# A four-block fp32 network on one core: convolution taps spread differently, LayerNorm means read from PSUM and squares summed on DVE, and the order of ACT's and PE's work in the differential-attention heads

## The reference

```python
def even_layer(x, ...):                       # SSD + conformer convolution
    z_a, xbc, dt_raw, glu_v, glu_g, z_b = split(rmsnorm(x) @ w_in)
    xs, bs, cs = split(silu(causal_dwconv(xbc, conv_w, conv_b)))
    y_a = rmsnorm_by_group(ssd_chunked(xs, dt, a, bs, cs, d_skip) * silu(z_a))
    u = causal_dwconv(glu_v * sigmoid(glu_g), dw_w, dw_b)     # 31 taps
    y_b = silu(layernorm(u, ln_w, ln_b)) * silu(z_b)
    return x + concatenate([y_a, y_b]) @ w_out

def odd_layer(x, positions, ...):             # differential attention, 8 heads
    q, k, v, gate = split(rmsnorm(x) @ w_in)
    q, k = rotary(rmsnorm(q)), rotary(rmsnorm(k))
    # two softmaxes a head, block-causal; 128 query rows at a time
    pr = softmax(mask(q @ k.T * scale))
    o = (pr[0] - lam * pr[1]) @ v
    o = rmsnorm(o, subln_w) * (1 - lam_init) * silu(gate)
    return x + o @ w_out
```

## Time and profile before

| | |
|---|---|
| time, median of 3 runs (lowest to highest) | 3186.87 us (3180.26 to 3199.41) |
| time of the profiled execution | 3183.37 us |
| its span in the profile | 3181.6 us |
| busy: PE, DVE, ACT, POOL | 95%, 59%, 30%, 25% of the span |
| mean granted clock of PE, share of full speed | 0.987 |

### The profile page before, as it was taken

How to read it: one execution, slowest core, us unless ns; L and a number is a source line. 1 busy time by engine, 2 the same in 40 slices (tenths; PEclk the granted TensorE clock), 3 DMA queues, 4 the chain that set the end, 5 groups by cost and what they waited for, 6 DMA issues and landing times. The chain is left out here.

```text
span 3181.6 us, 40107 instructions
## 1 busy us (share of the span) xinstructions
PE 3031.9 (95%) x16111; PEld 2452.0 (77%) x16111; DVE 1889.3 (59%) x2778; ACT 952.0 (30%) x1839; POOL 809.3 (25%) x466
## 2 busy tenths in 40 slices
PE   7999999889999999999999999998999999999898
PEld 6778787777788888888777777776687777777677
DVE  5334666534654254354588889898534566676673
ACT  3232444324210000011333343333312344444431
POOL 3222000241433333333233333232132211111111
PEclk9999999999999999999999999999999999999999
DMA  3012000110211111112211211124131110000011
GB/s 128 33 34 97 14 1 15 34 60 27 66 46 46 53 46 53 53 46 76 77 47 43 78 54 67 54 67 179 59 96 65 34 34 27 27 27 27 29 59 67
DMA packets 49281, 170.37 MB, mean 54 GB/s; under 512 B 5200, under 2 KB 5472, under 8 KB 48224
## 3 DMA queue, kind: packets, MB, share of 16 engines
q1 hardware_dynamic: 49120, 168.15, 15.7%
HBM read 145.06 MB, written 23.07 MB: 53 GB/s over the span
## 5 line engine op out<-in xcount | busy, mean ns | idle before, releaser
L194 PE MATMUL acc<-x_hi,w_hi 128*128 128x512 f32 x2048 | 824.1, 402 | 39.4 <-POOL w_lo L189 16.4
L187 POOL CAST w_hi<-w_raw 128x1024 fp32r<-128x1024 f32 x217 | 239.8, 1105 | 2318.8 <-PE acc L196 1374.5
L196 PE MATMUL acc<-x_hi,w_lo 128*128 128x512 f32 x2048 | 801.4, 391 | 0.0
L195 PE MATMUL acc<-x_lo,w_hi 128*128 128x512 f32 x2048 | 800.5, 391 | 0.0
L189 POOL TENSOR_TENSOR w_lo<-w_raw,w_hi 128x1024 fp32r<-128x1024 f32 x217 | 549.2, 2531 | 17.4
L194 PEld LDWEIGHTS acc<-x_hi,w_hi 128*128 128x128 f32 x2048 | 386.5, 189 | 131.4 <-issue 38.0
L196 PEld LDWEIGHTS acc<-x_hi,w_lo 128*128 128x128 f32 x2048 | 385.9, 188 | 82.6
L195 PEld LDWEIGHTS acc<-x_lo,w_hi 128*128 128x128 f32 x2048 | 386.9, 189 | 77.1 <-issue 2.4
L2569 DVE SCALAR_TENSOR_TENSOR acc<-ev_upad,cols,acc 128x1024 f32<-128x1024 f32 x232 | 298.5, 1287 | 5.4
L194 PE MATMUL aux<-x_hi,w_hi 128*128 128x512 f32 x464 | 197.8, 426 | 0.6 <-POOL w_lo L189 0.6
L196 PE MATMUL aux<-x_hi,w_lo 128*128 128x512 f32 x464 | 184.0, 397 | 0.0
(11 more groups left out here) (512 smaller groups left out, 5043.2 us busy)
## 6 DMA issues: line engine op xcount, KB each, us to landing
w_raw<-in_stream SPq DMA_DIRECT2D x217, 512.0 KB, 3.5
h<-in_x SPq DMA_DIRECT2D x16, 512.0 KB, 9.1
spill_h<-h SPq DMA_DIRECT2D x8, 512.0 KB, 5.3
spill<-ev_zst SPq DMA_DIRECT2D x8, 512.0 KB, 4.0
h_even<-spill_h SPq DMA_DIRECT2D x8, 512.0 KB, 11.7
ev_bz<-spill SPq DMA_DIRECT2D x8, 512.0 KB, 3.4
spill_h<-h_even SPq DMA_DIRECT2D x8, 512.0 KB, 5.4
h<-spill_h SPq DMA_DIRECT2D x8, 512.0 KB, 4.3
```

Of the source, the lines that this page charges most:

```text
L187: pool.tensor_copy(k.w_hi[slot][:], k.w_raw[slot][:]).then_inc(k.w_split, 1)
L194: pe.matmul(out, w_hi, x_hi, start=start, stop=False)
L195: pe.matmul(out, w_hi, x_lo, start=False, stop=False)
L196: return pe.matmul(out, w_lo, x_hi, start=False, stop=stop)
```

## The change

In the even block's groups, `conv(g, 1, ...)` has no taps inside it and four after it. The last group has fewer taps in its early part and in its chunks, and more after them, so that 3 of them stand ahead of `add(0)`. `total` moves from the middle of tile 2 to its last quarter. The mean is no longer copied: the centring is a `scalar_tensor_tensor` that reads the sums in PSUM. DVE adds the eight squares into one tile, so that `total_squares` is 2 matmuls, now in the last quarter of tile 4 instead of behind tile 3. The inverse root is written to PSUM and read there.

In the heads ACT reads the `zb` bank ahead of both exponents, `turn_o(h - 1, 0)` stands one quarter earlier, and the silu of the gate moves from t = 3 to t = 7. The last head's output is split in two halves.

```diff
-                    if c and between is not None:
-                        between()
                     for q in range(KD):
+                        if c and q == 4 and between is not None:
+                            between()
                         if c == 0:
...
             def total_squares():
-                pe.wait_ge(s["mean"], 1)
-                for j in range(KD):
-                    pe.wait_ge(s["sq_done"], j + 1)
-                    for c in (0, 1):
-                        mm = pe.matmul(S[c], k.ones, sq[j][:, c * HALF:(c + 1) * HALF], start=j == 0, stop=j == KD - 1)
+                pe.wait_ge(s["centred"], KD)
+                pe.wait_ge(s["q_sum"], KD - 1)
+                for c in (0, 1):
+                    mm = pe.matmul(S[c], k.ones, sq[0][:, c * HALF:(c + 1) * HALF], start=True, stop=True)
                 mm.then_inc(s["total2"], 1)
...
             first_pair()
             for i in range(2, KD):
-                out_tile(i, x_hi, x_lo, nothing, total if i == 2 else None)
-                if i == 3:
-                    total_squares()
+                out_tile(i, x_hi, x_lo, nothing, {2: total, 4: total_squares}.get(i))
...
@@ -2498,15 +2495,13 @@
             last_high(0)
             last_high(1)

-            act.wait_ge(s["total"], 1)
-            act.activation(mu[:], aux[:, 0:SEQ], ACT.Copy, scale=1.0 / D).then_inc(s["mean"], 1)
             for j in range(KD):
                 act.wait_ge(s["centred"], j + 1)
...
-            act.activation(rstd[:], rstd[:], ACT.Exp, scale=-0.5).then_inc(s["root"], 1)
+            act.activation(aux[:, 0:SEQ], rstd[:], ACT.Exp, scale=-0.5).then_inc(s["root"], 1)
...
-                    conv(g, 1, True)
-                    taps(1)
+                    conv(g, 1, False)
...
+                last = g == SSD_GROUPS - 1
                 conv(g, 3, False)
-                taps(5)
+                taps(3 if last else 5)
                 arrive(8)
                 mix(g, 0)
                 arrive(LEAD - 8)
...
                 n = per_chunk(g)
                 for c in range(TT):
-                    short = g == SSD_GROUPS - 1 and c >= 3
-                    taps(2 if short else 3)
+                    taps(2 if last else 3)
...
                     arrive(n // 3)
                     combine(g, c)
                     add_y(g, c)
                     arrive(n // 3)
-                    taps(0 if short else 2)
+                    taps(1 if last and c != 4 else 2)
...
             last_multiply(0)
-            taps(4)
+            taps(6)
             last_multiply(1)
             taps(1)
             sum_squares(SSD_GROUPS - 1)
-            taps(3)
+            taps(5)
             normalise(SSD_GROUPS - 1)
...
-            taps(CONF_K * KD - done[0] - 4)
...
             add(0)
-            taps(4)
+            taps(CONF_K * KD)
...
-            dve.wait_ge(s["mean"], 1)
+            dve.wait_ge(s["total"], 1)
             dve.wait_ge(s["tap"], CONF_K * KD)
+
+            def sum_of(j):
+                dve.wait_ge(s["sq_done"], j + 1)
+                if j > 1:
+                    dve.wait_ge(s["q_sum"], j - 1)
+                dve.tensor_tensor(sq[0][:], sq[0][:], sq[j][:], ALU.add).then_inc(s["q_sum"], 1)
+
             for j in range(KD):
-                dve.tensor_tensor(uc[:, j, :], uc[:, j, :], mu[:], ALU.subtract).then_inc(s["centred"], 1)
-                if j == 3:
+                dve.scalar_tensor_tensor(uc[:, j, :], aux[:, 0:SEQ], -1.0 / D, uc[:, j, :], ALU.mult, ALU.add).then_inc(s["centred"], 1)
+                if j == 4:
                     add(2)
+                if j >= 2:
+                    sum_of(j - 1)
+            sum_of(KD - 1)
             add(3)
             dve.wait_ge(s["root"], 2)
             dve.wait_ge(s["centred"], KD)
             for j in range(KD + 2):
                 if j < KD:
-                    dve.tensor_tensor(uc[:, j, :], uc[:, j, :], rstd[:], ALU.mult).then_inc(s["scaled"], 1)
+                    dve.tensor_tensor(uc[:, j, :], uc[:, j, :], aux[:, 0:SEQ], ALU.mult).then_inc(s["scaled"], 1)
                 if 1 <= j <= KD:
...
+                if h >= 1 and t == 2:
+                    turn_o(h - 1, 0)
                 quarter(1)
                 if h >= 1 and t == 2:
-                    turn_o(h - 1, 0)
                     turn_o(h - 1, 1)
                 if own:
...
-            pe.wait_ge(s["od_lo"], 8)
-            for r in range(2):
-                for c in range(2):
+            for c in range(2):
+                pe.wait_ge(s["od_lo"], H + c)
+                for r in range(2):
                     mm = output(rows[r][c], 4, r, c, range(3, 4))
-                mm.then_inc(k.lin_done if r else s["pieces"], 1)
+                    if c:
+                        mm.then_inc(k.lin_done if r else s["pieces"], 1)
...
                     take(("zf", h + 1, t), zts[t % 2])
-                if nxt:
-                    exponent(*nxt, 0)
                 if z and 1 <= t <= 4:
                     key = ("zb", h + 1, t - 1)
                     wait_full(act, key)
                     used(act.activation(qk[(h + 1) % 2][:, :, 256 * (t - 1):256 * t],
                                         bank(key).rearrange("p (j c) -> p j c", j=2), ACT.Copy), key)
                 if nxt:
+                    exponent(*nxt, 0)
                     exponent(*nxt, 1)
+                if fill and t == TT - 1:
+                    silu_gate(h + 2)
                 if own:
...
                     evacuate(h + 2, t // 2, t % 2)
-                    if t == 3:
-                        silu_gate(h + 2)
...
-            split_output(H - 1)
+            for c in range(2):
+                cols = slice(c * HALF, (c + 1) * HALF)
+                act.wait_ge(s["ring_dve"], USE[("o", H - 1, c)][2])
+                act.activation(d_hi[:, H - 1, cols], o[:, H - 1, cols], ACT.Copy).then_inc(s["od_hi"], 1)
...
-            lower_output(H - 1)
+            for c in range(2):
+                cols = slice(c * HALF, (c + 1) * HALF)
+                dve.wait_ge(s["od_hi"], H + c)
+                dve.tensor_tensor(d_lo[:, H - 1, cols], o[:, H - 1, cols], d_hi[:, H - 1, cols].bitcast(F32), ALU.subtract).then_inc(s["od_lo"], 1)
```

More of the change, by code:

```diff
@@ L1966, in block_even @@
     b_z = k.at("ev_bz", 96, [P, KD, SEQ])
-    mu, sq = k.at("ev_mu", 96, [P, SEQ]), [k.at(f"ev_sq{i}", 100 + 4 * i if i < 7 else 132, [P, SEQ]) for i in range(KD)]
+    sq = [k.at(f"ev_sq{i}", 100 + 4 * i if i < 7 else 132, [P, SEQ]) for i in range(KD)]
     rstd, zr = k.at("ev_rstd", 128, [P, SEQ]), [k.at(f"ev_zr{i}", 132 + 4 * i, [P, SEQ]) for i in (0, 1)]
@@ L1980, in block_even @@
              "state_ready chain yadded z_gated ymul squared sq_sum gtotal groot ynormed y_hi y_lo y_spilled ya_back h_back h_back0 "
-             "ya_back1 ya_back2 ya_back3 ya_back4 ya_back5 total mean centred sq_done total2 root scaled silued z_back gated b_hi b_lo added").split()
+             "ya_back1 ya_back2 ya_back3 ya_back4 ya_back5 q_sum total centred sq_done total2 root scaled silued z_back gated b_hi b_lo added").split()
     s = {n: k.own(f"e_{n}") for n in names}
@@ L2718, in _ @@
                     arrive(8)
-                    conv(g, 1, True)
-                    taps(1)
+                    conv(g, 1, False)
+                    taps(4)
                     arrive(8)
@@ L2730, in _ @@
                 arrive(LEAD - 8)
-                taps(4)
+                taps(2 if last else 4)
                 n = per_chunk(g)
                 for c in range(TT):
-                    short = g == SSD_GROUPS - 1 and c >= 3
-                    taps(2 if short else 3)
+                    taps(2 if last else 3)
                     if c + 1 < TT:
@@ L2753, in _ @@
             last_low(1)
-            taps(CONF_K * KD - done[0] - 4)
+            taps(min(3, CONF_K * KD - done[0]))
             def add(i):
```

1 line of the change is left out of this document (removed).

## The result

The changed kernel takes 3150.06 us, the median of 4 runs (3148.32 to 3157.71); the kernel before took 3192.91 in the 4 runs beside it (3180.26 to 3199.41). The ratio is 0.9877, 95% interval 0.9855 to 0.9899, so 32 to 46 us less. Measured again with more runs, the ratio was 0.9897 (0.9865 to 0.9930). The profiled execution took 3151.43 with a span of 3149.6, against 3183.37 and 3181.6.

What follows compares the result with a forecast made beforehand. PE, busy 95% of the span, was taken as the bound. Gains of 5.7 + 15.6 + 13.6 + 1.5 + 1.6 + 1.8 = 39.8 took the profiled 3183.4 to 3143.6, set at 3145 for run spread; range 3131 to 3164.

Steps and rivals of the forecast that it cites:

- SSD, -5.7: Even block's groups: 4.0 us of waits go at L2151, 2.2 at L2175; taps put back return 0.5.
- Tile 2, -8.2: Even block's output tile 2: starts 8.2 us earlier, at 2220.0, once POOL's split weights are ready.
- Squares, 12.1: Even block's norm: 4 records of squares' sums in place of 32 save 12.1 us of PE's work.
- the root 13.4 earlier: Even block's norm: the inverse root comes at 2268.2 to 2268.5, 13.4 us earlier than before.
- 2.1 + 12.1 - 0.2 = 14.0: Tile 2 to tile 8: half clock gone 2.1, squares 12.1, less PE's 0.2 us wait for DVE's sums.
- The wait at tile 8, 4.6 and 2 of clock: Output tile 8: PE waits 4.6 us for weights loaded and split behind the root, then loses 2 to half clock.
- The split `b_lo` isn't it: Tile 8: DVE's splits also follow the root but don't bind, since PE needs them one by one, 0.7 us apart.
- Heads, -13.6, -1.5 and -1.6: Odd block: t = 4, 2.10 us waits and half clock go, 0.65 waits come; t = 2, -1.5; heads 0 and 6, -0.4 and -1.2.
- Silu, 0: Heads, t = 7: the silu's 3.66 us stretch and the copy behind it stay covered by 1.5 us; no change.
- Tail, -1.8: Last head's output in halves: PE starts at 3136.4 instead of 3138.13, 1.8 us less, ends 0.5 to 3.4.
- the 3.3 that I had taken: Even block's norm: 3.3 us allowed for DVE being slowed where POOL works beside it.
- The "slower" rival: Heads, t = 1 to 4: zb reads delay the exponents, 28 places at 1.9 us, 53 in all, about 3197; chance 0.04.

Runs made afterwards that it cites:

- the second profile: The changed kernel as it is, measured and profiled again: 3156.24 us, ratio 0.9897 to the kernel before.
- the run of the zb read alone: The kernel before with one edit, ACT reading the zb bank ahead of both exponents: 3171.71 us, ratio 0.9941 to the kernel before.
- the first experiment: The changed kernel with four taps moved out of the last group's chunks to behind add(0): 3136.76 us.

## Why the prediction was right, and where not

The forecast was 3145 with a range of 3131 to 3164, and a gain of 39.8 on the profiled execution; measured were 3150.06, a gain of 31.9 between the profiled executions and 39 by the ratio. By the stretches it is 33.0. The SSD missed by 8.3, and heads and tail gave 3.0 more than their 18.5; that the whole time still came within 5 us is partly luck, as the part ahead of the even block alone varies by 20. Term by term, by the stretches:

- **SSD, -5.7: wrong in sign.** The first three groups gave 4.7 (I had 4.0 for L2151), but the last gave 7.4 back, +2.6 in all. The failed step is "*In the last group fewer taps stand in the chunks*" with the 0.5 that I took for the taps put back. That is not so, though the section on the change says it too. By the rows DVE did 12 taps between the last group's first and last `add_y` before, and does 21 now; fewer stand only from the group's first L2151 to the first `add_y` (10 instead of 15) and from there to the second (3 instead of 4), where L2175's waits were. In the chunks from c = 2 on DVE had none to two taps before, and so slack (it stood idle for 1.56 and 1.53 in two of them); with three its chunk is as long as PE's, and the two places where POOL's split stretches two DVE instructions by 3.0 us together become waits of 3.17 and 2.98 with the clock down behind. Taking two taps out ahead of each gave 9.2 to 9.9 back. The ends of this term, 3 to 6.5, were too narrow; I had named the risk, with no figure for it. The 4.7 of the first three groups fit the silu's ends, but no run takes that edit alone.
- **Tile 2, -8.2: right** to 0.1, with the cause named (1.0 on POOL's `w_lo`). The half clock behind it went too.
- **Squares, 12.1 and the root 13.4 earlier: right.** By the run with PE's sums the squares are worth 11.1. The root came 49.6 after PE had finished tile 1 (2222.66 to 2272.24), against 63.0 before (2218.96 to 2281.96), 13.4 sooner. From tile 2 to PE's arrival at tile 8 it is 81.8 after, 94.89 before: 13.1 less, where 2.1 + 12.1 - 0.2 = 14.0 was forecast.
- **The wait at tile 8, 4.6 and 2 of clock: right** at 4.17 and 2.9 (1.7 in the second profile). Its cause was half of the truth: `ev_blo` would hold PE as long. "*The split `b_lo` isn't it*" was wrong, at no cost to the sum.
- **Heads, -13.6, -1.5 and -1.6: mechanism right, size too small.** Measured -19.9 up to the tail's first product, of which 1.7 is the shorter tail wait; 18.2 against 16.7. The 2.10 went, the 0.65 came, the clock stayed up. Two edits of this part do nothing (the silu, and `turn_o` in the first heads), as the text had them, and `turn_o` costs 1.4 in the last two. Nearly all of the gain hangs on the zb read, which by itself gives a ratio of 0.9941.
- **Silu, 0: right.** ACT's stretch is 3.66 with no drain to be seen, and PE doesn't wait at t = 7. By the rule of the Trainium skill, "ScalarE: Activation LUTs", section "What ACT_TABLE_LOAD costs", it would be longer; these rows show none of the 1.38 after either load.
- **Tail, -1.8: right**, 1.2 to 1.8 by the run with the whole split. The two profiles differ by 3.3 there (1.7 of wait and 1.6 behind it), but the run of the zb read alone, with the tail of before, has 36.89 behind the wait instead of 37.89, so 1.0 of the 1.6 is clock that varies from run to run.
- **POOL beside DVE:** the Trainium skill, "SBUF — State Buffer", section "Who interferes with whom", has it that two SBUF inputs contend with a reading GpSimd and one input doesn't. The rows of the norm agree (1.21 for the centrings, 2.30 and 3.41 for the additions), and so do L2599 at 1.48 for 0.69 and L2610 at 2.58 for 0.42. I weighed the rule for the seven additions, where it cost the 3.3 that I had taken, and not for the SSD's chunks, where it decided.

The "slower" rival did not come: PE's one wait for the combined exponents (`diff_e`) is 2.0, and was 2.5 before.

## What to carry to other kernels

Moving work off one engine's busy place onto another place is priced by the slack at the new place, chunk by chunk, stretches by contention included, and not by an average over the stretch: a loop at the pace of its partner turns every hiccup into a wait. When a read frees a buffer for another engine, put it ahead of work that has its own wait; here an order of two lines was worth 17 to 19 us of 3187. And a wait that comes after one is removed can have two chains behind it, as at tile 8 here; look at both before moving a load. Count the instructions in both traces before saying that a stretch gets fewer of them: here the edited `taps(n)` suggested fewer, and the rows had more.

## What the runs showed of the hardware that I had not expected

The part ahead of the even block, the same in all kernels, ended between 1542 and 1562 us. In the window 400 to 800 us the granted clock was 1.00 in the run that ended it at 1542.75 and 0.96 in the one that ended it at 1562.47, and the same ACT instructions show the second run falling behind by 5.7 us ahead of this window and by 14.0 inside it, of 19.7 in all. So most of the spread of 20 us is clock granted in a stretch that the change doesn't touch. The window in the first experiment's run and in that of the zb read alone:

```profile
400.00:800.00 400.00, 363.20 (x2407) 306.33 (x2405) 224.11 (x355) 160.71 (x328) 77.98 (x41) 1.00 0.09 29
```

```profile
400.00:800.00 400.00, 363.06 (x2370) 307.62 (x2369) 211.16 (x353) 155.38 (x328) 65.97 (x34) 0.96 0.08 25
```

Behind the wait of 4.17 at tile 8 the clock stayed at 0.50 for three windows of 2 us (behind 4.18 in the second profile it was 1.00 in the third), behind waits of 0.65 and 1.26 in the heads it didn't fall, and behind the 3.17 in the last group it was back within some 4 us.
